# Second expert weights on ScalarE's DMA queue, first expert weights on SyncE's

## The reference

```python
def run_block(args):
    xblk, e = args
    return (jax.nn.silu(xblk @ w1[e]) * (xblk @ w3[e])) @ w2[e]
```

## Time and profile before

| | us |
|---|---|
| median of 3 runs | 1885.11 (1883.81 to 1886.62) |
| profiled execution, its own time | 1884.63 |
| its span, first to last instruction | 1882.8 |
| PE busy | 1758.7 (93% of the span) |
| DVE busy | 904.1 |
| ACT busy | 394.9 |
| DMA, mean over the span | 341 GB/s |

### The profile page before, as it was taken

The page is one execution under the profiler, slowest core; times in us unless marked ns, Lnnn a source line. Parts: engine busy times, 40 slices in busy tenths (PEclk is TensorE's granted clock), DMA queues, the critical chain, the costliest instruction groups (busy, mean ns, idle before and its releaser), DMA issues.

```text
span 1882.8 us, 26033 instructions
## 1 busy us (share of the span) xinstructions
PE 1758.7 (93%) x10270; PEld 1010.0 (54%) x10270; DVE 904.1 (48%) x1075; ACT 394.9 (21%) x465; POOL 17.1 (1%) x9
## 2 busy tenths in 40 slices
PE   1979999999999999998799999999999999999996
PEld 1868747786777777686434333343343433333341
DVE  5877766866757644446533333333233332323333
ACT  3010023432323233334111101111010111101011
POOL 0000000000000000001100000000000000000000
PEclk9989999999999999998899999999999999999998
DMA  9996596878868834554499999999999999999994
GB/s 374 386 387 238 208 379 261 325 280 333 326 265 302 312 138 175 190 193 164 199 422 422 422 422 422 422 422 422 422 422 422 422 421 422 422 422 422 422 422 185
DMA packets 140700, 641.92 MB, mean 341 GB/s; under 512 B 12658, under 2 KB 12786, under 8 KB 80114
## 3 DMA queue, kind: packets, MB, share of 16 engines
q1 hardware_dynamic: 139952, 637.08, 84.9%
q10 hardware_dynamic: 562, 2.55, 0.4%
q0 software_dynamic: 144, 1.70, 0.2%
HBM read 639.20 MB, written 2.10 MB: 341 GB/s over the span
## 4 chain that ended last, share of the span: by engine, by line
PE 51%; DMA 38%; DVE 8%; issue 1%; ACT 1%; SPq 1%; DVEq 0%; ACTq 0%
DMA ring<-in_exp_w 33%; PE ps L887 10%; PE ps L657 5%; PE ps L658 5%; PE ps L659 5%; PE ps L627 5%; DVE r_m L1174 4%; PE ps L851 3%; PE ps L570 3%; PE ps L583 3%; DMA ring<-in_branch_w 2%; DMA ring<-in_ada_w 2%; PE ps L752 1%; PE ps L753 1%; PE ps L754 1%; PE ps L874 1%
## 5 line engine op out<-in xcount | busy, mean ns | idle before, releaser
L887 PE MATMUL ps<-ring 128*64 128x512 f32 x2048 | 465.3, 596 | 16.9 <-DMA ring<-in_exp_w 16.9
L887 PEld LDWEIGHTS ps<-ring 128*64 128x64 f32 x2048 | 144.7, 137 | 303.6 <-issue 303.4
L1524 DVE TENSOR_TENSOR r_h<-r_h,ps 128x1024 f32<-128x1024 f32 x128 | 150.5, 1218 | 218.6 <-PE ps L874 218.5
L658 PE MATMUL ps<-g_lo,h_hi 128*128 128x512 f32 x512 | 202.4, 395 | 0.0
L1497 DVE TENSOR_TENSOR r_c<-ps,scale 128x512 f32<-128x512 f32 x65 | 44.7, 688 | 296.2 <-PE ps L829 296.2
L1100 ACT ACTIVATE r_m<-ps 128x512 f32<-128x512 f32 x32 | 19.1, 597 | 712.4 <-PE ps L887 712.4
L657 PE MATMUL ps<-mix_hi,h_hi 128*128 128x512 f32 x384 | 158.5, 413 | 0.0
L1027 ACT ACTIVATE mix_hi<-ring 128x1024 fp32r<-128x1024 f32 x96 | 101.7, 1062 | 260.6 <-PE ps L659 260.6
L1281 DVE TENSOR_TENSOR g_lo<-ring,mix_hi 128x1024 fp32r<-128x1024 f32 x96 | 117.5, 1225 | 79.5 <-ACT mix_hi L1027 78.2
L659 PE MATMUL ps<-mix_hi,h_lo 128*128 128x512 f32 x384 | 152.1, 396 | 0.0
L874 PE MATMUL ps<-ring,r_m 64*128 64x512 f32 x512 | 127.5, 615 | 1.4 <-DVE ring L1517 1.0
(11 more groups left out here) (242 smaller groups left out, 1749.2 us busy)
## 6 DMA issues: line engine op xcount, KB each, us to landing
ring<-in_exp_w SPq DMA_DIRECT2D x320, 1024.0 KB, 22.8
ring<-in_w_in SPq DMA_DIRECT2D x40, 2048.0 KB, 9.9
r_b<-in_exp_w SPq DMA_DIRECT2D x64, 1024.0 KB, 24.4
ring<-in_ada_w SPq DMA_DIRECT2D x24, 2048.0 KB, 18.8
ring<-in_ada_w SPq DMA_DIRECT2D x48, 1024.0 KB, 5.1
ring<-in_w_o SPq DMA_DIRECT2D x8, 2048.0 KB, 7.6
ring<-in_w_in SPq DMA_DIRECT2D x12, 1024.0 KB, 14.9
ring<-in_branch_w SPq DMA_DIRECT2D x6, 2048.0 KB, 9.6
```

The source lines that it names most:

```text
L658: mm(ps[:, b + t, :], h, lo[:, cols], start=False, stop=False)
L887: last = mm(ps[m * NWIN:(m + 1) * NWIN, 2, :], xe[:, k, :], chunk(2 * c + m)[:, kk * F:(kk + 1) * F], start=(k == 0), stop=(k == KT - 1))
L1524: V.tensor_tensor(x1n, x1n, ps[:, (6, 4)[b]:(6, 4)[b] + 2, :].rearrange("p b n -> p (b n)"), ALU.add).then_inc(added, 1)
```

## The change

SyncE's loop keeps the first weights only. A new function on ScalarE issues the four w2 chunks of pass p's expert, each as soon as TensorE has used that buffer in pass p: `4 * p + f + 5` is the count of `w2_used` that SyncE waited for one iteration later as `4 * (p + 1) + f + 1`. It is called between `copy_weights(p)` and `copy_hidden(p)`. The w2 chunks of pass 0 are still loaded by SyncE ahead of the loop.

```diff
@@ SyncE
             with sp.Fori(1, MAXPASS) as p:
                 with sp.If(p < n_pass):
-                    before = sp.value_load(etab[0:1, bass.ds(p - 1, 1)], min_val=0, max_val=NE - 1)
                     e = sp.value_load(etab[0:1, bass.ds(p, 1)], min_val=0, max_val=NE - 1)
                     for c in range(4):
-                        if c in (1, 2):
-                            with sp.If(p > 1):
-                                for f in (2 * c - 2, 2 * c - 1):
-                                    sp.wait_ge(w2_used, 4 * p + f + 1)
-                                    load_w2(before, f)
                         sp.wait_ge(w13_used, 4 * p + c + 1)
                         load_w13(e, c)
-            last_e = sp.value_load(etab[0:1, bass.ds(n_pass - 1, 1)], min_val=0, max_val=NE - 1)
-            for f in range(FT):
-                sp.wait_ge(w2_used, 4 * n_pass + f + 1)
-                load_w2(last_e, f)
@@ ScalarE
+            def load_next_w2(p):
+
+                e = act.value_load(etab[0:1, bass.ds(p, 1)], min_val=0, max_val=NE - 1)
+                for f in range(FT):
+                    act.wait_ge(w2_used, 4 * p + f + 5)
+                    act.dma_start(chunk(CHUNKS + f), e2_v[bass.ds(e, 1), :, f, :].rearrange("e p n -> (e p) n")
+                                  ).then_inc(w2_in[f], 16)
+
...
                     silu(p)
                     copy_weights(p)
+                    load_next_w2(p)
                     copy_hidden(p)
```

## The result

| | median us | runs | ratio to before |
|---|---|---|---|
| before | 1885.66 | 10 | |
| changed | 1890.69 | 10 | 1.0029, 95% interval 1.0020 to 1.0038 |

What follows compares the result with a forecast made beforehand. The prediction took TensorE's pace (28.95 us a pass) to bound the first passes and the DMA engines (29.82 us) the later ones. SP 0, ACT 0 and order of service +6.0 on 1885.11 gave 1891.1 us, range 1889.0 to 1893.5.

Steps and rivals of the forecast that it cites:

- The bound and the period: Expert stage: later passes go at the DMA engines' 422 GB/s, and the period stays 29.82 us after the change.
- SP and ACT cost nothing: Issue queues: four w2 issues a pass leave SP (0 us) and join ACT, which idles 22.76 us (0 us).
- Equal shares by packets: DMA engines: two queues alternate packet by packet, each at half the rate while w2 is outstanding, 4.97 us a chunk.
- No gain or loss of rate: Expert stage with both queues at work: total transfer rate unchanged, taken as 0; half a per cent would be 3.1 us.
- The rival in which two queues move more: Expert stage: a second queue fills gaps between chunks; with +1% rate 1881.9 us, at most 20.9 us less; chance 0.14.
- When the w2 queue starts: ACT's queue in each pass: 0.7 us from issue to data, so it works from 6.3 to 26.2 us after c0.
- the 5 to 10 that I gave as a sign: Sign of being right: w2 chunks land 5 to 10 us from their issue.
- From the last byte to the landing: End of the expert transfers: a chunk's last byte is 1.9 us before its landing.
- Which group is tied: First-weights groups in a pass: c0 and c3 both just in time, c1 and c2 early; last c3 6.0 us later.
- Taken once, early: Expert stage: the stall is taken in passes 2 to about 8, which ran at 28.95 us on slack.
- The tail moves whole: After the last c3: 38.6 us of dependent work keeps its length and moves by +6.0 us.
- The rival "nothing changes": Whole kernel: same engines, same bytes and a DMA-bound stage leave the time at 1885.1 us; chance 0.14.

Runs made afterwards that it cites:

- one_queue_act: Kernel before, with all expert weights from pass 2 on issued by ScalarE on one queue in SyncE's order; 1884.79 us, ratio 0.9997.
- mid_issue: The change, with w2 chunks 0 and 1 asked for after c1 of the pass, 2 and 3 after c3 and copy_hidden; 1888.55 us, ratio 1.0015.
- f01_act: The change with only w2 chunks 0 and 1 from ScalarE's queue, 2 and 3 staying with SyncE; 1889.82 us, ratio 1.0026.
- f23_act: The change with only w2 chunks 2 and 3 from ScalarE's queue, 0 and 1 staying with SyncE; 1889.20 us, ratio 1.0019.
- act_last4: The change with only the last four w2 sets (passes 28 to 31) from ScalarE's queue, SyncE's old order until then; 1892.06 us, ratio 1.0039.
- act_first15: The change with ScalarE's queue carrying w2 of passes 1 to 15 only, SyncE's old order from 16 to 31; 1885.53 us, ratio 1.0001.
- split_sp: Kernel before with each w2 chunk loaded by two DMAs of 4 KB rows, all from SyncE in the old order; 1892.50 us, ratio 1.0038.
- split_act: The change with each w2 chunk loaded by two DMAs of 4 KB rows on ScalarE's queue; 1898.60 us, ratio 1.0072.

## Why the prediction was right

**The bound and the period.** Right: 422 GB/s throughout, waits of 0.8 us once a pass, and 29.83 us from c0 to c0 over the 29 passes from 966.71 to 1831.78.

**SP and ACT cost nothing.** Right, and shown: one_queue_act with three times the issues is at +0.04 us.

**Equal shares by packets.** Right. After, from 1811 to 1830 us, when both queues have work:

```profile
q10 hardware_dynamic: 546, 4.08, 51.5%
q1 hardware_dynamic: 544, 3.93, 49.7%
```

**No gain or loss of rate.** Right to the resolution of the page. The rival in which two queues move more has nothing for it in any run.

**When the w2 queue starts.** Mis-sized. I had 0.7 us from issue to data, from an issue into idle engines; by packets even that one was 0.9 to 1.0, for none starts before 918.7 and three do by 918.8. Beside a busy queue it is 3.5. ScalarE's issues after, then q1 from 1837.4 to 1840.8, where q10 has no packet, and both from 1840.8 to 1841:

```profile
1837.32 2.06 ACTq L1097 DMA_DIRECT2D ring<-in_exp_w  x2
```
```profile
q1 hardware_dynamic: 192, 1.43, 101.2%
...
q10 hardware_dynamic: 7, 0.06, 68.4%
q1 hardware_dynamic: 3, 0.02, 29.5%
```

So the queue works from about 9.0 us after c0 (5.5 + 3.5) to about 28.7, not from 6.3 to 26.2. That is also why w2 takes 9.0 to 13.7 us from issue to landing, and not the 5 to 10 that I gave as a sign.

**From the last byte to the landing.** A wrong reading. I took 1.9 us, from the moment when the bulk of the last chunk was in. But its rows don't end together: 0.02 MB of it still start in 1852.6 to 1853 and it lands at 1853.4. The landings themselves are the safer measure, and the next point uses them.

**Which group is tied.** I found c0 and c3 both just in time; it is c0 alone. Landing of c0 in the last pass, before (L453, issued 1796.4 and 1796.9) and after (from the chain of waits: issue and time to landing), and of w2 chunk 3, issued 1817.7, and of c3, issued 1826.7 and 1827.1, after:

```profile
DMA to landing us min/median/max: 19.8/20.8/21.8
...
1806.19 25.46 DMA ring<-in_exp_w
...
DMA to landing us min/median/max: 13.7/13.7/13.7
...
DMA to landing us min/median/max: 20.2/22.5/24.8
```

Before, c0 lands at 1818.7, 900.85 us from the mark, after at 1831.65, 911.08 from it: 10.2 later. All four w2 chunks, issued behind it, are now served ahead of it (chunk 3 lands at 1831.4): 9.9 us, and 0.3 by which the last landing of the stage, too, is later. c0's slack before was 3.6 (it began at 1822.43, and 0.14 goes from landing to start). So c0 begins 6.6 later: 1831.78 - 920.57 = 911.21 for 904.61. From c0 to c3 it is 20.90 us after and was 21.75, because before had its wait at c2 in between; that gives 0.85 back and leaves the 5.75.

c3 lands at 1851.84, 5.6 us later than before by the mark, which is 2.2 chunks and not the 2.6 that I had. Less its slack of 0.5 that is 5.0, which c3 alone would have cost, and it has 0.7 us to spare. The prediction's 6.0 was worked out from c3, with too early a start of the queue, and it never worked out c0's lateness. That it came within 0.3 us of the 5.75 is luck in part: the mechanism and the place in the order of service were right, the group that sets the time was not. mid_issue, f01_act and f23_act, where another group is tied, are what separates the two.

**Taken once, early.** Right: c0 waits from pass 2 on. By the mark it begins 1.05 us later in pass 2 (966.71 for 962.91) and 1.9 later in pass 3 (996.52 for 991.86), gains another 0.87 a pass while the kernel before still runs its short passes, and has nearly all of the 6.6 by pass 9. act_last4 and act_first15 show that it is one delay, and not a charge for each pass.

**The tail moves whole.** Nearly: 37.8 us for 38.6. The first 16 matmuls of second(32) took 5.05 us, 5.86 before. They begin at the 1.2 GHz level in both, and it came back to the full one sooner; mean granted clock 0.73 in the six us from 1864 after, 0.64 in the six from 1856 before:

```profile
1864.00:1870.00 6.00, 6.00 (x22) 1.91 (x23) 0.05 (x1) 0.38 (x1) 0.00 (x0) 0.73 0.00 0
```
```profile
1856.00:1862.00 6.00, 6.00 (x18) 1.78 (x20) 0.00 (x0) 0.38 (x1) 0.00 (x0) 0.64 0.00 0
```

That size wanders from run to run without any change of the tail (4.89 in split_sp, 6.40 in split_act).

**The rival "nothing changes"** is excluded by the intervals of both series of the change. One thing about it was true, the period; the error would be to stop at the period.

## What to carry to other kernels

In this stage, bound by transfers and with single buffers, one queue in the order of use is not a bottleneck but the schedule. The second queue moved no more bytes a second; it only let later requests pass earlier ones, packet by packet, and the cost was the largest lateness over slack of any group, less the wait behind it that it replaced, and paid once. To size such a change list for each buffer the landing and the use, and for each one what can pass it; the group with the least slack (here c2, 0.0) need not be the one that is tied afterwards (c0, with 3.6, because four chunks pass it).

## What was not expected of the hardware

From a DMA's issue to its first packet took about 1 us into idle engines (917.82 to 918.8), and 3.4 to 3.6 us in each pass of the change, where q10 was empty and q1 kept all sixteen engines busy. What the time goes into, no run shows.

In a wait of 7 us on TensorE the granted clock fell to 0.50, the 1.2 GHz level, and 16 matmuls behind it took 5.0 us in place of 3.65.

Rows of 4 KB for a third of the bytes, in twice as many DMAs, cost 1% of the stage's rate (418 beside 422 GB/s).

The stage began at 916.3 to 920.6 us in the twelve profiled executions, although ahead of it they differ in nothing but the split of two early loads in the last two kernels: 4 us of scatter that a mark inside the stage takes out. From the medians alone +0.04 and +0.30 could not have been told from a microsecond either way.
